# A chunked RWKV scan whose 64 x 64 block products are confined to diagonal quadrants and grouped by tile form

## The reference, cut to what matters

```python
def rwkv7_scan(r, w, k, v, kk, bb, s0, reverse):
    def step(s, inp):
        r_t, w_t, k_t, v_t, kk_t, b_t = inp
        sa = jnp.einsum('bhij,bhj->bhi', s, kk_t)
        s = s * w_t[:, :, None, :] - sa[..., None] * b_t[:, :, None, :] + v_t[..., None] * k_t[:, :, None, :]
        return s, jnp.einsum('bhij,bhj->bhi', s, r_t)
```

## Time and profile before

| | us |
|---|---|
| median of 3 runs | 3610.51 (3607.00 to 3612.43) |
| the profiled execution | 3614.98 |
| its span on the core | 3613.2 |
| PE busy / PEld busy in the span | 3264.3 / 2621.8 |
| DVE / ACT / POOL busy | 1643.0 / 1210.0 / 1371.4 |
| mean granted clock of TensorE | 0.939 of full |
| the 36 steps of the scan (2477.4 to about 3020) | some 543 |

### The profile page before, as it was taken

How to read it: one execution, slowest core, us unless ns; L and a number is a source line. 1 busy time by engine, 2 the same in 40 slices (tenths; PEclk the granted TensorE clock), 3 DMA queues, 4 the chain that set the end, 5 groups by cost and what they waited for, 6 DMA issues and landing times. The chain is left out here.

```text
span 3613.2 us, 46690 instructions
## 1 busy us (share of the span) xinstructions
PE 3264.3 (90%) x17343; PEld 2621.8 (73%) x17343; DVE 1643.0 (45%) x2965; ACT 1210.0 (33%) x2105; POOL 1371.4 (38%) x936
## 2 busy tenths in 40 slices
PE   6999998899989999898999789945999997989996
PEld 5888775688868887676888678824777775768875
DVE  6443385444345654225311254043666645364443
ACT  3222344322233222343222222233444433234342
POOL 3444331344434443323444312245666630123332
PEclk8999999899989999898999889967999998969998
DMA  7555331455536543223333312222222224111211
GB/s 227 186 184 159 99 91 35 139 183 183 159 109 186 165 144 124 74 65 110 117 97 93 112 41 59 88 77 56 68 68 62 62 55 156 30 46 54 58 53 41
DMA packets 634369, 371.98 MB, mean 103 GB/s; under 512 B 69711, under 2 KB 626757, under 8 KB 633697
## 3 DMA queue, kind: packets, MB, share of 16 engines
q1 hardware_dynamic: 629984, 362.58, 33.5%
q10 hardware_dynamic: 3056, 6.29, 0.5%
q0 software_dynamic: 1168, 0.91, 0.1%
HBM read 343.23 MB, written 26.50 MB: 102 GB/s over the span
## 5 line engine op out<-in xcount | busy, mean ns | idle before, releaser
L266 POOL TENSOR_TENSOR w_lo<-w_raw,w_hi 128x1024 fp32r<-128x1024 f32 (+1 forms) x398 | 939.3, 2361 | 1854.4 <-ACT w_hi L258 1854.4
L303 PE MATMUL acc<-h,w_hi 128*128 128x512 f32 x3136 | 979.1, 393 | 6.5 <-POOL w_lo L266 6.5
L258 ACT ACTIVATE w_hi<-w_raw 128x1024 fp32r<-128x1024 f32 (+1 forms) x398 | 414.4, 1042 | 996.9 <-PE acc L303 961.1
L303 PEld LDWEIGHTS acc<-h,w_hi 128*128 128x128 f32 x3136 | 584.2, 188 | 128.5 <-POOL w_lo L266 7.6
L303 PE MATMUL acc<-h,w_lo 128*128 128x512 f32 x1568 | 613.3, 391 | 0.0
L303 PE MATMUL acc<-hid,w_hi 128*128 128x512 f32 x1408 | 437.0, 392 | 0.0
L303 PE MATMUL lat<-h,w_hi 128*128 128x512 f32 x992 | 367.9, 408 | 15.9 <-DVE h L428 13.8
L303 PEld LDWEIGHTS acc<-h,w_lo 128*128 128x128 f32 x1568 | 294.9, 188 | 64.0
L707 DVE SCALAR_TENSOR_TENSOR ada_part<-ada_raw,c_act,ada_part 128x256 f32<-128x256 f32 x672 | 315.0, 488 | 18.6
L303 PEld LDWEIGHTS acc<-hid,w_hi 128*128 128x128 f32 x1408 | 263.5, 188 | 54.1
L303 PE MATMUL acc<-hid,w_lo 128*128 128x512 f32 x704 | 275.0, 391 | 0.0
(11 more groups left out here) (484 smaller groups left out, 5052.5 us busy)
## 6 DMA issues: line engine op xcount, KB each, us to landing
w_raw<-in_ffn_w SPq DMA_DIRECT2D x240, 512.0 KB, 3.8
ada_raw<-in_ada_w SPq DMA_DIRECT2D x88, 1024.0 KB, 4.9
image<-inverse_wait SPq DMA_DIRECT2D x144, 128.0 KB, 2.3
w_raw<-in_od_w_in SPq DMA_DIRECT2D x32, 512.0 KB, 4.0
w_raw<-in_ev_w_in SPq DMA_DIRECT2D x30, 512.0 KB, 3.8
w_raw<-in_ffn_w SPq DMA_DIRECT2D x32, 384.0 KB, 3.1
low_wait<-w_raw SPq DMA_DIRECT2D x36, 256.0 KB, 2.3
first_ada<-in_ada_w SPq DMA_DIRECT2D x8, 1024.0 KB, 12.3
```

The source lines that it names most:

```text
L258: act.activation(K.w_hi[:, first % SPLIT, 0:tiles, :], K.raw[:, first % RAW, 0:tiles, :], ACT.Copy).then_inc(K.hi_ready, 1)
L266: pool.tensor_tensor(K.w_lo[:, first % SPLIT, 0:tiles, :], K.raw[:, first % RAW, 0:tiles, :], K.w_hi[:, first % SPLIT, 0:tiles, :].bitcast ...
L303: mm = pe.matmul(out, w[:, slot, k, :], moving(ap, k, tokens), start=first and k == 0 and p == 0, stop=last and k == tiles - 1 and p == le ...
```

## The change

- `cross`, `join` and the transposes of `turn` run on the two diagonal quadrants alone: per head one product on rows and columns 0 to 63 and one on 64 to 127, 64 columns wide. Both write bank 0 (`turn`: bank 1) of `wide`, each its own half of the partitions. `turn`'s transposes become plain matmuls with the identity.
- `image`, `level`, `x` and `y` shrink to 64 columns per head. An image load is 8 DMAs of 32 KB (64 partitions x 2 heads x 64 columns) in place of 4 of 128 KB.
- ACT's copy of the transposed x to `t` takes the late half alone; the early half is copied by DVE, a new operation that is the chunk's fifth DA signal. `close` waits for it, and so does the next image load. t's fourth quadrant is cleared once by POOL at the start.
- TensorE's order: both `take` products before the transposes (`tokens`), `cross` before slot 1, the state's product of `read` apart (`recall`), both `read`, both `join`, slot 3, then `write`, `turn`, `turn`, `write`. On DVE slot 3 and `add(0)` come after both `join` parts, followed by the new copies.

```diff
-    HALVES = ((slice(0, 64), slice(64, 128)), (slice(64, 128), slice(0, 64)))
-    PA, AA, DA, PS, AS, DS = 7, 6, 4, 4, 2, 3
+    SIDES = (slice(0, 64), slice(64, 128))
+    HALVES = (SIDES, SIDES[::-1])
+    PA, AA, DA, PS, AS, DS = 7, 6, 5, 4, 2, 3
...
-                tok=S.sb("tok", [P, 2, 3, P]), y=S.sb("y", [P, 2, P]), x=S.sb("x", [P, 2, P]),
-                t=S.sb("t", [P, 2, 2, P]), image=S.sb("image", [P, 2, 2, P]),
+                tok=S.sb("tok", [P, 2, 3, P]), y=S.sb("y", [P, 2, 64]), x=S.sb("x", [P, 2, 64]),
+                t=S.sb("t", [P, 2, 2, P]), image=S.sb("image", [P, 2, 2, 64]),
...
-                sp.dma_start(level[:], A["levels"][10:12].rearrange("d t s -> t d s")).then_inc(S.tables, 16)
+                for a in SIDES:
+                    sp.dma_start(level[a], A["levels"][10:12, a, a].rearrange("d t s -> t d s")).then_inc(S.tables, 16)
...
-                        for form in range(2):
-                            sp.dma_start(V.image[:, form], K.inverse_dram[form, d, k, :, 0:CH * CH].rearrange(
-                                "h (t s) -> t h s", t=CH)).then_inc(V.image_in, 16)
+                        for a in SIDES:
+                            for form in range(2):
+                                sp.dma_start(V.image[a, form], K.inverse_dram[form, d, k, :, 0:CH * CH].rearrange(
+                                    "h (t s) -> t h s", t=CH)[a, :, a]).then_inc(V.image_in, 16)
...
+                for n, (V, (early, late)) in enumerate(zip(U, HALVES)):
+                    pool.wait_ge(S.zeros, 3 + n)
+                    pool.memset(V.t[late, :, :, early], 0.0).then_inc(S.zeros, 1)
...
+
+                    def tokens(d):
+                        V, way = U[d], cols(d, k)
                         pe.transpose(V.wide[:, 0, 2 * P:3 * P], u[:, c + 2 * RB, way], K.ident)
                         pe.transpose(V.wide[:, 0, 3 * P:4 * P], O.kt[d][:, way], K.ident)
                         pe.transpose(V.wide[:, 1, 2 * P:3 * P], O.rate[d][:, way], K.ident).then_inc(V.pa, 1)
...
-                        pe.wait_ge(V.image_in, total(c, k, 32, 32))
+                        pe.wait_ge(V.image_in, total(c, k, 64, 64))
                         for h in range(2):
-                            mm = pe.matmul(V.wide[:, 0, h * P:h * P + P], V.bq[:, h, :], V.image[:, 0, h, :],
-                                           start=True, stop=True)
+                            for a in SIDES:
+                                mm = pe.matmul(V.wide[a, 0, h * 64:h * 64 + 64], V.bq[a, h, a], V.image[a, 0, h, :],
+                                               start=True, stop=True)
                         mm.then_inc(V.pa, 1)
...
                         for h in range(2):
-                            mm = pe.matmul(V.wide[:, 0, h * P:h * P + P], V.image[:, 1, h, :], V.y[:, h, :],
-                                           start=True, stop=True)
+                            for a in SIDES:
+                                mm = pe.matmul(V.wide[a, 0, h * 64:h * 64 + 64], V.image[a, 1, h, :], V.y[a, h, :],
+                                               start=True, stop=True)
                         mm.then_inc(V.pa, 1)
...
                         for h in range(2):
-                            mm = pe.transpose(V.wide[:, 1, h * P:h * P + P], V.x[:, h, :], K.ident)
+                            for a in SIDES:
+                                mm = pe.matmul(V.wide[a, 1, h * 64:h * 64 + 64], V.x[a, h, :], K.ident[a, a],
+                                               start=True, stop=True)
                         mm.then_inc(V.pa, 1)
...
-                            mm = pe.matmul(V.wide[late, 0, h * 64:h * 64 + 64], V.bq[early, h, late], V.x[early, h, early],
+                            mm = pe.matmul(V.wide[late, 0, h * 64:h * 64 + 64], V.bq[early, h, late], V.x[early, h, :],
...
+                        pe.wait_ge(V.da, total(c, k, DA, 5))
...
-                    def read(d):
+                    def recall(d):
                         V, way = U[d], cols(d, k)
                         pe.wait_ge(V.ac, total(b, k, AS, 2))
+                        pe.matmul(V.low[:, 2 * P:3 * P], V.s[:], O.cs[d][:, way], start=True, stop=False)
+
+                    def read(d):
+                        V = U[d]
                         out = V.low[:, 2 * P:3 * P]
-                        pe.matmul(out, V.s[:], O.cs[d][:, way], start=True, stop=False)
...
                     take(0)
                     take(1)
+                    tokens(0)
+                    tokens(1)
...
                     keys(1)
                     solve(0)
                     solve(1)
-                    between(1)
                     cross(0)
                     cross(1)
+                    between(1)
+                    recall(0)
+                    recall(1)
                     between(2)
                     read(0)
+                    read(1)
                     join(0)
-                    write(0)
                     join(1)
                     between(3)
-                    read(1)
+                    write(0)
                     turn(0)
+                    turn(1)
                     write(1)
-                    turn(1)
                     between(4)
                     close(0)
                     close(1)
...
                         act.wait_ge(V.pa, total(c, k, PA, 5))
-                        act.activation(V.t[:, buf], V.wide[:, 1, 0:2 * P].rearrange("p (h t) -> p h t", h=2),
...
                         act.wait_ge(V.pa, total(c, k, PA, 6))
-                        act.activation(V.y[late, :, 0:64], V.wide[late, 0, 0:P].rearrange("p (h t) -> p h t", h=2),
...
-                        dve.tensor_tensor(V.y[:], V.wide[:, 0, 0:2 * P].rearrange("p (h t) -> p h t", h=2),
+                        dve.tensor_tensor(V.y[:], V.wide[:, 0, 0:P].rearrange("p (h t) -> p h t", h=2),
...
-                        dve.tensor_tensor(V.x[:], V.image[:, 0], V.wide[:, 0, 0:2 * P].rearrange("p (h t) -> p h t", h=2),
+                        dve.tensor_tensor(V.x[:], V.image[:, 0], V.wide[:, 0, 0:P].rearrange("p (h t) -> p h t", h=2),
...
+                    def turn(d):
+                        V, (early, late) = U[d], HALVES[d]
+                        dve.wait_ge(V.pa, total(c, k, PA, 5))
+                        dve.tensor_copy(V.t[early, buf, :, early], V.wide[early, 1, 0:P].rearrange(
+                            "p (h t) -> p h t", h=2)).then_inc(V.da, 1)
...
                     cross(1)
                     between(2)
                     join(0)
-                    add(b, k, 0)
                     join(1)
                     between(3)
+                    add(b, k, 0)
+                    turn(0)
+                    turn(1)
                     add(b, k, 1)
                     between(4)
                     between(5)
```

More of the change, by code:

```diff
@@ L1927, in even_scan_phase @@
         masks = S.sb("masks", [P, 4, P])
-        level = S.sb("level", [P, 2, P])
+        level = S.sb("level", [P, 2, 64])
         lw = S.sb("lora_w", [P, 4, P])
@@ L1968, in heads @@
         def heads(ap):
-            return ap.rearrange("p (a c) -> p a c", a=1).broadcast_to([P, 2, P])
+            return ap.rearrange("p (a c) -> p a c", a=1).broadcast_to([P, 2, ap.shape[1]])
         def cols(d, k):
@@ L2046, in scatter @@
                         for V in U:
-                            sp.wait_ge(V.image_in, total(c, 0, 32))
+                            sp.wait_ge(V.image_in, total(c, 0, 64))
                     for d in range(2):
@@ L2142, in prepare @@
                         op(f"kw{d}", O.kt[d], O.kt[d], wi[d], ALU.mult, ("pool", "ksum"))
-                pool.wait_ge(S.tables, 48)
+                pool.wait_ge(S.tables, 64)
                 prepare(0)
@@ L2250, in close @@
                         pe.wait_ge(V.aa, total(c, k, AA, 5))
+                        pe.wait_ge(V.da, total(c, k, DA, 5))
                         for h in range(2):
-                            mm = pe.matmul(V.wide[early, 1, h * 64:h * 64 + 64], V.y[late, h, 0:64], V.t[late, buf, h, late],
+                            mm = pe.matmul(V.wide[early, 1, h * 64:h * 64 + 64], V.y[late, h, :], V.t[late, buf, h, late],
                                            start=True, stop=True)
                         mm.then_inc(V.pa, 1)
-                    return take, keys, cross, join, turn, close
+                    return take, tokens, keys, cross, join, turn, close
                 def state_parts(b, k):
@@ L2297, in write @@
                         pe.matmul(out, V.tok[:, buf, 2, :], V.sa[:], start=False, stop=True).then_inc(V.ps, 1)
-                    return right, solve, read, write
+                    return right, solve, recall, read, write
                 def ready(c):
@@ L2305, in begin @@
                     ready(0)
+                    pe.wait_ge(S.zeros, 5)
                     for part in chunk_parts((0, 0)):
@@ L2311, in step @@
                     nxt = following(b, k)
```

(20 more changed lines are left out.)

## The result

| | before | after |
|---|---|---|
| median of 12 runs each | 3608.98 (3603.48 to 3620.18) | 3618.19 (3614.14 to 3633.64) |
| ratio, 95% interval | | 1.0027 [1.0014, 1.0040] |
| profiled execution: span, mean granted clock | 3613.2, 0.939 | 3619.2, 0.932 |

The change is slower by 0.27%, some 9 us. I had given 3574.

The account below looks back on a forecast made before the run. TensorE's own stream was taken to set the pace in all but two of six steps. Terms -34.4 - 4 - 1 + 2 + 2.5 - 1 = -36 us took 3615.0 to 3579 profiled, 3574 median; range 3556 to 3604.

Parts of the forecast that it names:

- Price of a diagonal pair: On TensorE, two diagonal quadrant products run together at 0.058 us a pair; in turns they would take 0.116.
- rival 1: On TensorE the two quadrants of a pair take turns, giving 3619 us, slower than before; chance 0.13.
- A plain step, -1.14: Ordinary scan steps, without inversion products or special waits, get 1.14 us shorter each.
- The wait for ACT before `close`: TensorE's 0.27 us wait per plain step for ACT's copy goes, covered by `write(1)` and a change of form.
- (b,0), -1.86: Step 0 of blocks 0 to 4, with inversion products: 1.86 us less each, 0.72 of it from fewer form changes.
- (b,2), -1.0 each: Step 2 of blocks 0 to 3, which waits on DVE: 1.0 us less each, bounds -1.4 and +0.5.
- images "in time by 1 us": In a plain step the last image load lands at 15.9 us, before the next step's second `cross` at 16.9.
- eight issues of 0.5: SP issues a chunk's eight image loads at 0.5 us each, from 10.1 to 13.6 us into a plain step.
- (b,1), -0.3 each: Step 1 of blocks 0 to 3: 0.3 us less each despite a 1.5 us lora_w wait; total -1, bounds -1.5 and +1.
- Rival 3: Steps 1 and 2 of the blocks hit their upper bounds and the clock falls longer, 3591 us; chance 0.09.
- Rival 2: Image loads come late in every step because 256-byte runs issue and land 1 us slower, 3604 us; chance 0.08.
- +0.15 of a plain step: With both `take` parts together, each needs its direction's last ACT copy sooner, adding 0.15 us to a plain step.

Follow-up runs that it names:

- e10: e7 with SyncE issuing a chunk's images when x is made, not after DVE's copy of t; 3576.8 us, ratio 0.9912 to the kernel before.
- e12: The changed kernel, its 8 image loads kept, with the images issued when x is made, not after DVE's copy of t; 3599.7 us, ratio 0.9972.
- e7: The changed kernel with its compact images loaded by 4 DMAs of 128 partitions, not 8 of 64, from a DRAM copy with rows of 64; 3580.7 us.

## Why the prediction was wrong

- **Price of a diagonal pair: right.** It costs 0.054 (0.058 forecast), and `cross` with its change 0.61 in e10. The work saved by order and quadrants together was under-sized: some 50 us at full clock, by the estimate above, for some 38 by the forecast's terms (1.02 in each of 34 steps, 0.72 in five). "TensorEngine Tiling (Array Packing)" of the Trainium skill, under "Gotcha 1: PSUM Pressure", would have had the pairs take turns, and rival 1 and its 3619 with them. The time came out near that number, but by another mechanism: the trace contradicts the rule for diagonal pairs in one bank.
- **A plain step, -1.14: right in block 5 (11.2 to 11.4), but by two misses that cancel.** The stream saves 1.5 (11.0 in e10 and e12), and the late image takes some 0.35 back in `cross`. The wait for ACT before `close` is gone there, as forecast. Of my signs, (5,1) with 11.4 and the pairs 7 ns apart came true; `cross` spans 0.97 and not 0.5, and PE waited 13 times for the image.
- **(b,0), -1.86: right**, 14.6 for 16.6, -2.0.
- **(b,2), -1.0 each: the gain was twice that**, -2.0. About half of it is clock (the low clock took 8.3 us of these four steps before and 4.4 after, by their mean clocks). In e10, where (b,1) is short, it is -1.0 each; that the longer (b,1) gave DVE's chain more time would fit, and is not shown.
- **The step that failed is the images "in time by 1 us", with its term "eight issues of 0.5".** I took the median issue of the earlier trace rows, of loads of 128 partitions, for loads of 64. They cost 0.607 and follow each other in 0.65, so a chunk's images hold SP for 5.1 us, not 4. The trace of before could have told it: its lora_w loads are of 64 partitions, and by line (ns min/median/max) they had cost 0.6 us there:

```profile
L2023 SPq DMA_DIRECT2D lora_w<-in_ev_a x12: 590/597/1217, 2362.5 to 2796.9; - x12
```

  With it the margin of 1 us was gone by arithmetic: 10.1 + 7 x 0.65 + 2.1 = 16.8, against 16.9. What happened in (5,1): the images were issued from 10.5 us into the step, not 10.1, the last at 15.0, not 13.6, and the second `cross` started 17.2 into it, 0.3 after it was due. With the loads cheap (e7) or begun earlier (e12) this wait is gone in block 5.
- **(b,1), -0.3 each: it became +4.1.** The last lora_w load came at 12.5, not at 8.7: two chunks' images stand ahead of the sends, each started from DVE's copy (3.9 us later than before), and the gather waited 2.1 us more for the sends. PE was there at 9.5, as forecast, and waited 5.0 for a forecast of 1.5. Its bound of +1 a step was far too narrow, since it held no case in which the whole queue is late.
- **Missed: a wait can be paid twice.** After the waits the granted clock is at 0.50 for some microseconds, which costs some 17 us more than in the kernel before, by the estimate above. Rival 3 had the clock at 1 us a step, but not as what follows from SP's waits.
- Rival 2 (images late, 3604, 0.08) was nearest in kind. Its reason was wrong (256-byte runs; the landing did not change) and it left out lora_w behind the images, so it fell short by 14 us.
- Two sums of the rivals are off: case 1 leaves out the +0.15 of a plain step (35 steps, so 3624 and not 3619), and case 3 adds up to -17, 3593 and not 3591. Neither changes which case came nearest.

With SyncE's two causes taken away the total comes out: e10's scan is 36.7 us under that of before and its median 3576.8, for a forecast of -36 and 3574. In part that is luck. By groups (b,0) gave 13.7 for 9.3 and (b,1) 5.7 for 1, while (b,3) to (b,5) gave 7.1 for 13.7 and (4,1) to (4,5) 0.3 for 5.7. And by the weighting above e10 has the same 50.5 us less work as the change, of which waits (8.7 more than before) and clock (5.2) take 14 back.

## What to carry to other kernels

Cost a DMA's issue by a row of the same shape, and then walk its queue to the end: what stands behind the doubled loads, by when is it due, and from which signal does the queue start. Halving the bytes of a load bought nothing here, where its issues doubled; lay the DRAM side out so that one load still covers all 128 partitions. Before moving a load forward in a queue, name the due time of what it is moved ahead of, and of the engine with the longest unbroken run of work behind it.

## What the runs showed of the hardware

- Issue time on SyncE (median ns) by the partitions of the SBUF side: loads of 128x2x128 469, 128x2x64 468, 128x1x128 432; of 64x2x128 607, 64x2x64 607, lora_w's 64x128 597; scatters from 48 partitions 486, from every second of 48 (24) 766. It follows neither the bytes nor the partitions alone; why 64 is dearer than 48 was not tried.
- Diagonal 64x64 quadrants that write two partition halves of one PSUM bank run together, and `turn`'s transposes run even among the products of the next line in another quadrant, a few tens of ns apart.
- The granted clock halves at times after a wait of one or two microseconds, and then PE works at half speed for five to seven. In e10 a wait of 1.10 us ahead of `keys` in step (2,4) was followed by this (windows of 1 us, as above):

```profile
2724.00:2725.00 1.00, 0.20 (x2) 0.20 (x4) 0.42 (x1) 1.00 (x6) 1.00 (x2) 1.00 0.78 128
2725.00:2726.00 1.00, 0.98 (x8) 0.40 (x6) 0.87 (x2) 1.00 (x4) 1.00 (x1) 1.00 0.88 137
2726.00:2727.00 1.00, 1.00 (x10) 0.84 (x6) 0.94 (x2) 0.14 (x2) 0.86 (x2) 0.79 0.02 3
2727.00:2728.00 1.00, 1.00 (x10) 0.88 (x11) 0.00 (x0) 0.42 (x3) 1.00 (x1) 0.50 0.00 0
```

PE is busy throughout until 2733 at 0.50, some 3 us lost for a wait of 1.1; the step took 19.8 us, where the same step of other blocks took 13 to 14.5. In that block GpSimd was 1 us later than in the others; why one wait brings the clock down and another does not stays open (in the change, PE waited 1.64 us ahead of 2721.62, and step (2,2) behind it had a clock of 1.00).
